# Attention in a streaming encoder step: TensorE computes a slice's scores before its values, and ScalarE runs the sigmoids before it empties the finished outputs

## What is computed

```python
# differential attention: 4 heads, two 64-wide maps each
s = where(visible, q.k * 64**-0.5 - slope*|distance|, NEG_INF)
p = softmax(s);  a = p[map 0] - lam * p[map 1];  o = a @ v          # then a norm per head
# stick-breaking attention: 8 heads of 64, strictly causal
z = q.k * 64**-0.5
a = exp(log_sigmoid(z) + sum over later keys of log_sigmoid(-z));  o = a @ v
# h = x + w_out[o_diff | o_stick];  y = h + SwiGLU(norm(h));  final norm
```

## Time and profile before

| | |
|---|---|
| median of three runs | 1430.06 us (1428.70 to 1430.52) |
| the profiled execution | 1428.36 us |
| its span, first to last instruction | 1426.6 us |
| mean granted TensorE clock | 0.987 of full speed |
| attention, first to last matmul | 281.6 to 592.2 us |

### The profile page before, as it was taken

The page is one execution under the profiler, slowest core; times in us unless marked ns, Lnnn a source line. Parts: engine busy times, 40 slices in busy tenths (PEclk is TensorE's granted clock), DMA queues, the critical chain, the costliest instruction groups (busy, mean ns, idle before and its releaser), DMA issues.

```text
span 1426.6 us, 23794 instructions
## 1 busy us (share of the span) xinstructions
PE 1370.9 (96%) x9152; PEld 1200.4 (84%) x9152; DVE 1003.2 (70%) x1323; ACT 624.2 (44%) x1109; POOL 452.1 (32%) x404
## 2 busy tenths in 40 slices
PE   6999999889999999899979999999999999999997
PEld 5778888668888777688779999999999998788886
DVE  5996958598877889756688665667766657754466
ACT  6634333278887877323342222321322233543343
POOL 2333330100010000011155544544543554644344
PEclk9999999989999999899989999999999999999999
DMA  7365540365544445433224334444433447944554
GB/s 248 110 236 179 191 155 34 116 173 141 139 125 120 122 123 161 132 125 124 72 91 172 126 130 148 142 148 167 164 110 132 169 142 278 322 165 163 166 187 170
DMA packets 172200, 218.05 MB, mean 153 GB/s; under 512 B 19836, under 2 KB 110328, under 8 KB 170680
## 3 DMA queue, kind: packets, MB, share of 16 engines
q1 hardware_dynamic: 163416, 193.13, 41.7%
q0 software_dynamic: 3840, 12.58, 2.7%
q10 hardware_dynamic: 4832, 10.82, 2.0%
HBM read 152.98 MB, written 63.50 MB: 152 GB/s over the span
## 4 chain that ended last, share of the span: by engine, by line
PE 47%; DMA 1%; DVE 1%; issue 1%; SPq 0%; ACT 0%; POOLq 0%; POOL 0%; ACTq 0%; DVEq 0%
PE ps_feed L2859 11%; PE ps_feed L2860 11%; PE ps_feed L2861 11%; PE ps_feed L2890 4%; PE ps_feed L2889 4%; PE ps_feed L2888 4%; PE ps_feed L2904 1%; PE ps_feed L2905 1%; DMA aux<-in_w_down 1%; DMA s_dram<-blocks 0%; DVE parts_early L2727 0%; SPq L2414 0%; DVE blocks L2705 0%; DVE blocks L2706 0%; SPq L2432 0%
## 5 line engine op out<-in xcount | busy, mean ns | idle before, releaser
L727 PE MATMUL ps_proj<-shared 128*128 128x512 f32 x224 | 90.0, 402 | 3.4 <-DVE shared L583 2.1
L1670 PE MATMUL ps_aT<-ident,z 128*128 128x128 f32 (+1 forms) x568 | 84.6, 283 | 5.5 <-DVE z L1513 5.4
L728 PE MATMUL ps_proj<-shared 128*128 128x512 f32 x224 | 88.1, 393 | 0.0
L2540 ACT COPY aux<-ps_feed 128x544 f32<-128x544 f32 x22 | 13.5, 615 | 170.3 <-PE ps_feed L2861 170.3
L729 PE MATMUL ps_proj<-shared 128*128 128x512 f32 x224 | 88.0, 393 | 0.0
L1345 ACT COPY aT<-ps_aT 128x512 f32<-128x512 f32 (+2 forms) x168 | 81.2, 524 | 15.6 <-PE ps_aT L1670 14.5
L2490 POOL TENSOR_TENSOR ring_more<-staging,ring_more 128x512 fp32r<-128x512 f32 x45 | 69.6, 1550 | 56.4 <-ACT ring_more L2526 56.3
L2490 POOL TENSOR_TENSOR shared<-staging,shared 128x512 fp32r<-128x512 f32 x41 | 60.0, 1469 | 86.1 <-ACT shared L2526 86.1
L2754 DVE TENSOR_TENSOR blocks<-ps_feed,blocks 128x512 f32<-128x512 f32 x56 | 36.0, 683 | 66.2 <-PE ps_feed L2890 66.2
L1513 DVE TENSOR_TENSOR_SCAN z<-z,near 128x1024 f32<-128x1024 f32 (+7 forms) x64 | 81.5, 1336 | 0.0
L1670 PEld LDWEIGHTS ps_aT<-ident,z 128*128 128x128 f32 (+1 forms) x568 | 64.7, 144 | 17.4 <-DVE z L1513 7.1
(11 more groups left out here) (354 smaller groups left out, 4536.7 us busy)
## 6 DMA issues: line engine op xcount, KB each, us to landing
staging<-s_dram SPq DMA_DIRECT2D x50, 256.0 KB, 3.6
staging<-in_w_gate SPq DMA_DIRECT2D x11, 1024.0 KB, 7.8
blocks<-in_w_up SPq DMA_DIRECT2D x11, 1024.0 KB, 5.4
blocks<-in_w_down SPq DMA_DIRECT2D x11, 1024.0 KB, 9.8
t_dram<-blocks SPq DMA_DIRECT2D x11, 1024.0 KB, 3.9
s_dram<-blocks SPq DMA_DIRECT2D x11, 1024.0 KB, 5.2
w_raw<-in_w_in SPq DMA_DIRECT2D x10, 1024.0 KB, 6.4
staging<-in_cache_sb_v POOLq DMA_DIRECT2D x31, 256.0 KB, 3.3
```

The lines of the kernel that those rows point to most:

```text
L727: nc.tensor.matmul(res, a_hi[:, k, cols], b_hi[:, k], start=start, stop=False)
L728: nc.tensor.matmul(res, a_hi[:, k, cols], b_lo[:, k], start=False, stop=False)
L1670: last = nc.tensor.transpose(ps_aT[0:m, G % 2, k], z(x, at, m), t["ident"][:, :])
```

## The change

Two blocks of code move. On TensorE, `score` goes ahead of `values` in each slice. On ScalarE, `keep` goes ahead of `output` in the first slice of an iteration; `keep` exists only for the stick-breaking steps, so this matters from iteration 17 on. The numbering of the banks in the ring, the semaphores and all instructions stay.

```diff
@@ ScalarE, in the loop over i and s @@
-                    if 0 <= i - 1 and s == 0:
-                        output(i - 1)
                     for j in slots:
                         if SB0 <= i + SCORE < NSTEP and j < len(units(i + SCORE)):
                             keep(i + SCORE, j)
+                    if 0 <= i - 1 and s == 0:
+                        output(i - 1)
@@ TensorE, in the loop over i and s @@
                     for j in turned_now:
                         turn(i, j)
+                    for j in slots:
+                        if 0 <= i + SCORE < NSTEP and j < len(units(i + SCORE)):
+                            score(i + SCORE, j)
                     for j in turned_now:
                         if grp0[i] + j >= LAG:
                             values(grp0[i] + j - LAG)
                     for j in slots:
                         if i == NSTEP and j < LAG:
                             values(len(owner) - LAG + j)
-                    for j in slots:
-                        if 0 <= i + SCORE < NSTEP and j < len(units(i + SCORE)):
-                            score(i + SCORE, j)
```

## The result

The changed kernel takes 1434.81 us in the median of nine runs (1431.18 to 1439.42), against 1430.06 us for nine runs of the kernel before. The ratio is 1.0041, with a 95% interval of 1.0027 to 1.0055: slower by 0.4%, just above the range I gave. Its profiled execution took 1431.18 us, with a span of 1429.4 us and a mean granted clock of 0.989. Three executions, two of the kernel before in the series with a median of 1430.11 us (1523 and 7585 us) and one of pe_stick (2250 us), were slow; they stand in the medians and not in the ratios.

A forecast was written before the change was run, and what follows sets the result against it. TensorE was taken to bound attention up to 541 us, VectorE's scans after. Terms 0.45 + 0.9 - 0.9 + 0.1 = +0.55 us on the profiled 1428.36 gave 1428.9; median forecast 1430.7 us, range 1427.2 to 1434.6.

The forecast's parts named there:

- The differential heads: Attention iterations 2 to 16, three heads: net +0.3 us per head, +0.9 us in all.
- late second units: Differential heads: second score unit waits for its bank, freed late after prepared keys; 0.8 us per head of five iterations.
- relief of old waits: Differential heads: new lateness and the keys' old 0.20 us wait are largely one delay; 0.5 us back per head.
- other changes of shape: TensorE's switches between matmul shapes: three per slice in either order; taken as 0, bounds 0.05 us a slice.
- stick-breaking bound: Stick-breaking heads: upper bound on lateness less lead, about 0.2 us for each of 16 iterations, 3.2.
- The slower rival: Differential heads: late score units stall TensorE in full, 0.5 us in four of five iterations; about +5 us, 1435; chance 0.2.
- The first iteration: At 307.68 us TensorE's 0.51 us wait for a read of scores grows, values come after it; +0.45 us.
- The change-over: Iteration 17: sigmoids ahead of outputs and full clock bring the turning of 429.28 us earlier by 1.0, less 0.1: -0.9 us.
- The clock: At 424 to 428 us: stays up after a 1.5 us wait; with the fall, the change-over is about -0.2.
- The stick-breaking heads: Iterations after 17: first-slice values are shorter and the lead covers what is missing; +0.1 us for all four heads.
- ScalarE's new order: After iteration 17: outputs come two sigmoids later but are needed later still; costs nothing.
- The signs: Changed profile: L1414 waits of 0.2 to 0.4 us, L1331 wait 1.2 to 1.5, clock near 1.00, iteration 25 unchanged.

The follow-up runs named there:

- pe_stick: Kernel before with only TensorE's scores ahead of values, from iteration 17 on; ScalarE as before: 1442.02 us, ratio 1.0089.
- values_first: Kernel before with TensorE's values ahead of turnings, then scores, up to iteration 16; ScalarE as before: 1433.17 us, ratio 1.0027.
- keys_early: Kernel before with TensorE's order turning, scores, prepared keys, values up to iteration 16; ScalarE as before: 1431.66 us, one run.
- keep_iteration: Kernel before with TensorE's scores ahead of values up to iteration 16, except iterations 5, 10 and 15: 1433.81 us, one run.
- stick_both: Kernel before with ScalarE's sigmoids ahead of outputs, and TensorE's scores ahead of values only from iteration 17 on: 1430.24 us, ratio 1.0004.
- pe_diff: Kernel before with only TensorE's scores ahead of values, in iterations below 17; ScalarE as before: 1433.15 us, ratio 1.0030.
- later_slices: Kernel before with TensorE's scores ahead of values only in second and third slices, up to iteration 16: 1435.25 us, one run.
- keep_sample: Kernel before with TensorE's scores ahead of values up to iteration 16, except first slices of iterations 5, 10, 15: 1435.10 us, ratio 1.0042.
- first_slice: Kernel before with TensorE's scores ahead of values only in the first slice of iterations up to 16: 1431.71 us, one run.
- keys_early_sample: Kernel before with turning, scores, keys, values up to iteration 16, but values before scores in first slices of 5, 10, 15: 1432.75 us, ratio 1.0028.
- pe_only: Kernel before with only TensorE's scores ahead of values, in every slice; ScalarE as before: 1444.52 us, ratio 1.0111.
- values_first_keep: Kernel before with TensorE's values, turning, scores up to iteration 16, but iterations 5, 10, 15 as before: 1429.46 us, one run.

## Why the prediction was wrong

**The differential heads** are the step that failed. I had +0.8 us a head for late second units, less 0.5 of relief, +0.9 us in all for three heads; it is +3.85, about 1.3 a head. Iterations 7 to 11 lost 1.23. By the lengths from start to start in the changed kernel and the one before, they divide so:

| us in a head | forecast | measured, iterations 7 to 11 |
|---|---|---|
| late second units | +0.8 | +1.05 |
| relief of old waits | -0.5 | -0.57 |
| the sample's last block | not in the sum | +0.30 |
| other changes of shape | 0 | +0.45 |

- *Late units.* The mechanism was right and the size low. The scores of the first slice are longer by 0.31 us in iteration 7 and 0.53 in iteration 8, where I had 0.27 and 0.35, and by 0.21 in iteration 10. In values_first, with turnings ahead of the scores and values behind them as in the changed kernel but no late unit, they take 1.58 and 1.09 us in iterations 7 and 8, as before, so the 0.31 and 0.53 are not shape. keys_early took 1.8 us back by an earlier bank.
- *The relief* came, in about the size that I had taken: 0.23 us at the keys of iteration 7, 0.14 at those of iteration 11, and 0.20 in iteration 10, where in the kernel before the third unit's load waited for the read of the first (row below). Still, the new delay of iteration 7 and the old one are not one and the same, as I had put it: one came and the other went. And VectorE did have a gap there, 0.15 us at 352.45.
- *The sample's last block* was not in my sum. I read only changes of shape between full groups; this one did not exist before, since block and scores were of one height. It is 0.30 us a head.
- *Changes of shape otherwise*, which I set to 0 with 0.05 us a slice as the bound. They are what is left, 0.45 us a head or 0.04 for each of its 11 slices with turnings: turnings behind keys or values and ahead of scores take 0.09 us longer, 0.04 in the second slice, and only part of it comes back. In values_first it was 0.04 to 0.08 an iteration in most. The bound was right and 0 was not.

```profile
374.44 0.22 PEld L1650 LDWEIGHTS ps_z<-shared 64*128 64x128 f32 x2 [0.30 <-DVE lowest L1469]
```

The late units are seen from both sides, in the rows and in a run that moves the bank. The other three are differences of rows alone: no run takes out the relief, the block or the shapes by itself. keep_iteration fits: the 0.44 us of iteration 10 went, and with it the 0.17 that iteration 11 had gained, 0.27 net, about a third of the 0.85 by which that kernel lost less.

In the recorded sums, the 3.2 us of the stick-breaking bound takes 0.2 for the lateness less the lead, which is 0.27, and the sum gives 1430.6, not 1430.7. Neither changes the outcome.

**The slower rival** had the place and the size (1435), but not quite the cause: it needed 0.5 us in four of five iterations and no relief. There were 0.31, 0.53 and 0.21 us in three, and the rest came from the block and the changes of shape.

**The first iteration**: 0.45 forecast, 0.54 measured, but stick_both has 0.53 there with the old order. The agreement is not shown to be more than luck.

**The change-over** had the right sign, but only thanks to the clock. ScalarE in the changed kernel:

```profile
424.04 0.18 ACT L1319 ACTIVATION_READ_ACCUMULATOR z<-z,lowest 128x1 f32 x1
424.24 1.28 ACT L1331 ACT_TABLE_LOAD   x1
425.54 1.94 ACT L1331 ACTIVATE z<-ps_z 128x1024 f32<-128x1024 f32 x2
```

TensorE behind it:

```profile
426.71 0.39 PE L1650 MATMUL ps_z<-shared 64*128 64x256 f32 x2 [1.50 <-ACT z L1331]
...
432.71 0.49 PE L1670 MATMUL ps_aT<-ident,z 128*128 128x128 f32 x3
```

The table load stands right behind the exponential, the wait is the 1.5 us forecast, and the turning of 429.28 is at 432.71, 1.14 us earlier once the 4.57 us by which the first turning of iteration 17 was late are taken off; I had 1.0 less 0.1, and -0.9 for the whole change-over. What I missed comes an iteration later: the sample's scores (L1639) wait 0.5 us for the last keys' low part, its slice lost 0.8 us, and -0.37 is left. And it is all the clock's: pe_diff, with the old order at this place and a clock that did not fall, has its turning 1.64 us earlier and keeps -1.64 to iteration 20. At one clock the new order is 0.5 us slower up to that turning and 1.3 us slower up to iteration 20.

**The clock** came out as forecast, by luck as far as the runs show. I argued from the wait's length (1.50 against 1.70 us). In pe_diff the wait was still 1.70 us, and the clock did not fall:

```profile
426.56 0.39 PE L1650 MATMUL ps_z<-shared 64*128 64x256 f32 x2 [1.70 <-ACT z L1331]
```

```profile
426.00:436.00 10.00, 9.15 (x81) 8.21 (x82) 2.21 (x6) 8.35 (x17) 0.00 (x0) 1.00 0.53 127
```

**The stick-breaking heads** came to +0.32 where I had 0.1, and iteration 25 kept its length (7.25 us before and now), so unseen scores-to-values changes cost nothing that shows there:

```profile
487.31 1.09 PE L1670 MATMUL ps_aT<-ident,z 128*128 128x128 f32 x8
488.33 0.39 PE L1650 MATMUL ps_z<-kT_hi,qT_hi 64*128 64x256 f32 x2
...
488.89 1.09 PE L1703 MATMUL ps_o<-aT,v 128*64 128x128 f32 x16
489.92 0.44 PE L1670 MATMUL ps_aT<-ident,z 128*128 128x128 f32 x2
```

That ScalarE's new order costs nothing was right. That it is what keeps TensorE's from costing 8.3 us I had not seen; I had costed the two halves one by one. VectorE is busy all of 557 to 572 us as foreseen.

**The signs** that I had named for being right came true: waits of 0.3 us for L1414, 1.5 us for L1331, full clock at 424 to 428 us, iteration 25 of unchanged length. They were signs of the mechanism and said little of its size, most of which no list of waits shows.

## What to carry to other kernels

- Where engines share a small ring in program order, list the slack of every tenant, not only of the one that the edit brings nearer: here a third unit had 0.30 us, and the order of later_slices, which leaves the second one's distance alone, starved the third. Sum lateness and relief place by place, from start to start, and not from the list of waits.
- Count the neighbours of the odd-sized blocks too. The sample's half-height block cost 0.3 us more between full-height matmuls than beside others of its height.
- When two engines' lists move together, write out the cycle (scores, sigmoid, output, values): one half alone can be far worse than both (8.3 us against 0.3 here).

## What the runs showed of the hardware

- The same wait of 1.69 to 1.71 us at iteration 17 was followed by half clock (1.2 of 2.4 GHz) in four profiled executions (before, keep_sample, keys_early, keep_iteration) and by full clock in four (pe_diff, first_slice, later_slices, keys_early_sample). Waits of 1.19 to 1.50 us kept full clock in all four that had them. Of the longer ones, 2.01 us (values_first) and 2.81 us (pe_only and pe_stick) were followed by half clock and 2.10 us (values_first_keep) was not. The two outcomes are 1.7 us apart (pe_diff's -1.64 against keys_early's +0.02). What decides it stays open; the length alone does not.
- The profile's list of waits shows 0.27 us where a late weight load cost 0.44 from start to start, for the load also loses its lead over the matmul (0.03 us, where it was 0.17). Differences of starts are the surer measure.
